# Gating layer of a decoder trunk: one column block of u computed with both parts of x as one moving operand

## The reference, cut to what matters

```python
def mixer_sgu(x, w_in, b_in, ln_g, ln_b, w_s, b_s, w_out):
    h = jax.nn.gelu(x @ w_in + b_in)               # (256, 2048)
    u, v = jnp.split(h, 2, axis=-1)                # 1024 columns each
    v = layer_norm(v, ln_g, ln_b)
    v = v.reshape(B, nc, SGU_CHUNK, SGU_GROUPS, gw)  # 2 chunks of 128 tokens, 8 groups of 128 channels
    w = jnp.where(causal, w_s, 0)
    mixed = jnp.einsum('gts,bcsgd->bctgd', w, v) + b_s.T[None, None, :, :, None]
    y = u * mixed.reshape(B, S, SGU_WIDTH)
    return y @ w_out
```

## Time and profile before

| what | us |
|---|---|
| median of three runs | 998.92 |
| the profiled execution's own time | 998.7 |
| its span in the trace | 997.0 |
| TensorE busy | 991.9 (99% of the span) |
| TensorE weight loads busy | 850.7 (85%) |
| VectorE busy | 703.7 (71%) |
| ScalarE busy | 458.3 (46%) |

### The profile page before, as it was taken

One profiled execution on the slowest core, in us unless ns is written; L12 is line 12 of the kernel. 1 busy time (PEld: TensorE's weight loads), 2 busy tenths in 40 slices (PEclk: granted clock), 3 DMA queues, 4 the chain that ended last, 5 costly groups with the idle time before them and its releaser, 6 DMA issues.

```text
span 997.0 us, 13952 instructions
## 1 busy us (share of the span) xinstructions
PE 991.9 (99%) x5370; PEld 850.7 (85%) x5370; DVE 703.7 (71%) x876; ACT 458.3 (46%) x524; POOL 49.7 (5%) x74
## 2 busy tenths in 40 slices
PE   9999999999999999999999999999999999999998
PEld 7888888889878888888888888888898888888887
DVE  5866666878678766666786666668787876666684
ACT  5444344246574544444445443434354553434441
POOL 0700000100001000000010000000210000000010
PEclk9999999999999999999999999999999999999999
DMA  8965656466264675555457755555466676565531
GB/s 289 289 234 168 211 168 212 133 191 185 85 212 164 201 245 192 188 191 194 143 170 270 230 183 201 180 199 182 145 205 218 215 243 213 168 212 171 211 128 43
DMA packets 129799, 191.45 MB, mean 192 GB/s; under 512 B 5448, under 2 KB 95816, under 8 KB 129760
## 3 DMA queue, kind: packets, MB, share of 16 engines
q1 hardware_dynamic: 126432, 180.11, 54.5%
q0 software_dynamic: 3040, 10.54, 3.1%
q10 hardware_dynamic: 288, 0.26, 0.1%
HBM read 189.83 MB, written 1.06 MB: 191 GB/s over the span
## 4 chain that ended last, share of the span: by engine, by line
PE 99%; DMA 0%; DVE 0%; issue 0%; DVEq 0%
PE gu L619 26%; PE gu L627 14%; PE acc L435 10%; PE acc L436 10%; PE acc L437 10%; PE gu L435 6%; PE gu L437 5%; PE gu L436 5%; PE tp L534 2%; PE gu L829 2%; PE gu L919 2%; PE gu L810 2%; PE gu L834 1%; PE gu L924 1%; PE gu L813 1%; PE acc L754 1%
## 5 line engine op out<-in xcount | busy, mean ns | idle before, releaser
L619 PE MATMUL gu<-xT,g_hi 128*128 128x512 f32 x1152 | 274.6, 390 | 0.0
L619 PEld LDWEIGHTS gu<-xT,g_hi 128*128 128x128 f32 x1152 | 215.5, 188 | 44.5 <-ACT g_hi L987 0.2
L1472 DVE TENSOR_REDUCE stage<-gu 128x256 f32<-128x512 f32 x72 | 49.8, 691 | 146.0 <-PE gu L627 146.0
L627 PEld LDWEIGHTS gu<-xT,g_lo 128*128 128x128 f32 x1152 | 147.7, 191 | 5.6
L627 PE MATMUL gu<-xT,g_lo 128*128 128x256 f32 x1152 | 149.4, 283 | 0.0
L1323 DVE TENSOR_TENSOR g_lo<-rawA,g_hi 128x2048 fp32r<-128x2048 f32 (+2 forms) x63 | 136.8, 2173 | 17.4 <-ACT g_hi L987 17.2
L1323 DVE TENSOR_TENSOR g_lo<-rawB,g_hi 128x2048 fp32r<-128x2048 f32 (+1 forms) x64 | 136.5, 2134 | 7.4 <-ACT g_hi L987 7.3
L435 PE MATMUL acc<-d_hi,hT_hi 128*128 128x512 f32 x352 | 138.6, 394 | 0.0
L436 PE MATMUL acc<-d_lo,hT_hi 128*128 128x512 f32 x352 | 137.9, 392 | 0.0
L437 PE MATMUL acc<-d_hi,hT_lo 128*128 128x512 f32 x352 | 137.0, 389 | 0.0
L987 ACT ACTIVATE g_hi<-rawA 128x2048 fp32r<-128x2048 f32 (+2 forms) x64 | 116.0, 1816 | 40.6 <-DMA rawA<-in_ffn_w_up 16.0
(11 more groups left out here) (205 smaller groups left out, 1020.9 us busy)
## 6 DMA issues: line engine op xcount, KB each, us to landing
rawD<-in_ffn_w_down SPq DMA_DIRECT2D x44, 1024.0 KB, 5.5
rawA<-in_ffn_w_gate SPq DMA_DIRECT2D x42, 512.0 KB, 4.0
rawA<-in_ffn_w_up SPq DMA_DIRECT2D x42, 512.0 KB, 5.0
rawB<-in_ffn_w_gate SPq DMA_DIRECT2D x42, 512.0 KB, 4.0
rawB<-in_ffn_w_up SPq DMA_DIRECT2D x42, 512.0 KB, 5.0
rawA<-in_attn_w_in SPq DMA_DIRECT2D x12, 512.0 KB, 4.4
rawB<-in_attn_w_in SPq DMA_DIRECT2D x12, 512.0 KB, 4.5
rawA<-in_ple_w_gate SPq DMA_DIRECT2D x8, 512.0 KB, 4.8
```

Of the source, the lines that this page charges most:

```text
L619: pe.matmul(bank[:, :], g_hi[:, slot, b, at:at + P], xT[:, b, :, :].rearrange("p i t -> p (i t)"), start=b == 0, stop=False)
L627: done = pe.matmul(bank[:, 0:S], g_lo[:, slot, b, at:at + P], xT[:, b, 0, :], start=False, stop=b == KB - 1)
L1472: dve.tensor_reduce(gates, gu[0][:, :].rearrange("p (i t) -> p t i", i=2), AXX, ALU.add).then_inc(gate_sum, 1)
```

## The change

The pieces n = 4 and n = 5 (chunk c = 2, the first column block of u) use a new function `u_wide`. It puts the two channel blocks of a piece into the two banks, and multiplies each high weight with both parts of x in one matmul of 512 columns; the low weights follow in a second pass of 256 columns. VectorE adds the halves of each bank (`u_sum`) into `stage`, and ScalarE's gelu reads `stage` (`gelu_sum`) and signals `u_ready`. The sums of n = 4 stand inside the norm of half 0, between its two steps; the sums of n = 5 and both low parts of chunk g0 + 3 stand ahead of the statistics of half 1. Pieces 6 and 7 stay as they were.

```diff
-           "sgu": dict(g=6, d=0, u=4, t=2, v=2, a=4, x=4, r=4, ln=2),
+           "sgu": dict(g=6, d=0, u=5, t=2, v=2, a=4, x=4, r=4, ln=2),
@@ tensor
+                    def u_wide(c, h):
+
+                        slot = (g0 + c) % 2
+                        for n, (wait, w) in enumerate((((high_a, high_b), g_hi), ((split_a, split_b), g_lo))):
+                            for i_b in range(2):
+                                if n == 0:
+                                    pe.wait_ge(gu_taken[i_b], u0 + c + h)
+                                at = P * (2 * h + i_b)
+                                for b in range(KB):
+                                    if h == 0 and i_b == 0 and b % 4 == 0:
+                                        pe.wait_ge(wait[b // 4], g0 + c)
+                                    if n == 0:
+                                        pe.matmul(gu[i_b][:, :], w[:, slot, b, at:at + P],
+                                                  xT[:, b, :, :].rearrange("p i t -> p (i t)"), start=b == 0, stop=False)
+                                    else:
+                                        done = pe.matmul(gu[i_b][:, 0:S], w[:, slot, b, at:at + P], xT[:, b, 0, :],
+                                                         start=False, stop=b == KB - 1)
+                                if n == 1:
+                                    done.then_inc((wide_full, g_done)[i_b], 1)
+
                     for n, (c, h) in enumerate((c, h) for c in range(4) for h in range(2)):
-                        bank_free(n % 2, u0 + n // 2)
+                        if n < 4:
+                            bank_free(n % 2, u0 + n // 2)
+                        elif n > 5:
+                            bank_free(n % 2, u0 + 4)
...
+                        elif c == 2:
+                            u_wide(c, h)
                         else:
                             u_product(c, h)
@@ scalar
+                    def gelu_sum(h):
+
+                        for i_b in range(2):
+                            act.wait_ge(gu_taken[i_b], u0 + 3 + h)
+                            done = act.activation(uT[:, 2 * h + i_b, :], stage[:, i_b, S * h:S * h + S],
+                                                  ACT.Gelu_apprx_tanh, bias=bu_col[:, 2 * h + i_b:2 * h + i_b + 1])
+                        done.then_inc(u_ready, 1)
+
-                    gelu_u(4)
-                    gelu_u(5)
+                    gelu_sum(0)
+                    gelu_sum(1)
@@ vector
-            def ln_apply_row(src, dst, h, ln, ready):
+            def ln_apply_row(src, dst, h, ln, ready, between=None):
...
                 steps[0] += 2
+                if between is not None:
+                    between()
                 dve.wait_ge(rstd_ready, 2 * ln + h + 1)
...
+                    def u_sum(h, i_b):
+
+                        dve.wait_ge(*((wide_full, 2 * WIDE + h + 1), (g_done, 2 * g0 + 5 + h))[i_b])
+                        if h == 0:
+                            dve.wait_ge(act_done, a0 + 3 + i_b)
+                        dve.tensor_reduce(stage[:, i_b, S * h:S * h + S],
+                                          gu[i_b][:, :].rearrange("p (i t) -> p t i", i=2), AXX, ALU.add)\
+                            .then_inc(gu_taken[i_b], 1)
+
+                    def u_sums():
+                        u_sum(0, 0)
+                        u_sum(0, 1)
...
-                        for bank in range(2):
-                            dve.wait_ge(gu_taken[bank], u0 + 3 + j)
+                        if j == 0:
+                            dve.wait_ge(u_ready, 2)
+                        else:
+                            for bank in range(2):
+                                dve.wait_ge(gu_taken[bank], u0 + 5)
...
                     ln_stats(v_sgu[:, 0, :], 0)
                     biased(3, 1)
-                    ln_apply_row(v_sgu[:, 0, :], v_sgu[:, 0, :], 0, ln0, vn_ready)
+                    ln_apply_row(v_sgu[:, 0, :], v_sgu[:, 0, :], 0, ln0, vn_ready, between=u_sums)
+                    lo_g(g0 + 3, 0)
+                    lo_g(g0 + 3, 1)
+                    u_sum(1, 0)
+                    u_sum(1, 1)
                     dve.wait_ge(act_done, a0 + 4)
                     ln_stats(v_sgu[:, 1, :], 1)
-                    lo_g(g0 + 3, 0)
-                    lo_g(g0 + 3, 1)
                     ln_apply_row(v_sgu[:, 1, :], v_sgu[:, 1, :], 1, ln0, vn_ready)
```

More of the change, by code:

```diff
@@ L277, in build @@
         wide_full = sem("wide_full")
+        u_ready = sem("u_ready")
         y_ready, y_high, y_low = sem("y_ready"), sem("y_high"), sem("y_low")
```

## The result

Twenty executions each: median 1000.49 us against 998.67 us before, 1.82 us more, a ratio of 1.0024 with a 95% interval of 1.0018 to 1.003. The forecast was 1000.4 us, 1.5 above the 998.92 that the first three executions of the kernel before had given; the range was 999.5 to 1001.5. The profiled execution took 1000.43 us, 1.7 more than the one before, and its span is 998.7 against 997.0.

A forecast was written before the change was run, and what follows sets the result against it. The prediction took TensorE, busy for 99% of the span, to bound the kernel. Its terms, -0.42 + 1.79 + 0.12 = +1.49 us, on 998.92 us gave 1000.4 us, with a range of 999.5 to 1001.5.

The forecast's parts named there:

- Part 1: Matmuls of n = 4 and 5: two pieces in the 512-column form save 0.42 us.
- Part 2: In n = 4, TensorE waits 1.68 us for biased(3, 1) to free bank 1, plus 0.11 restart: 1.79 us.
- Parts 3 and 4: From n = 4 to 5, waiting for bank 0 costs 0.12 us; from n = 5 to 6, mixing hides VectorE's work, cost 0.
- the tie of part 3: Ahead of n = 5, bank 0 is freed at 737.94 and TensorE wants it at 738.00; 0.12 us taken.
- Part 5: Behind n = 6: later norm, gate and w_out loads stay hidden, cost 0; g0 + 5's first half keeps 0.3 us cover.
- a late load of w_out: In the stage's later loads: a w_out load landing late would show the forecast wrong.
- n = 6 did not wait: Rival ahead of n = 6: a longer VectorE list makes bank 0 late, in sum +1.9 us, 1000.8 us; chance 0.12.
- the late-half rival: Rival at w_out: g0 + 5's first half lands late, +1.0 us, in sum +2.5, 1001.4 us; chance 0.16.
- The gain if the wait were gone: Rival in n = 4: bank 1 is free by 732.5, leaving -0.30 us, 998.6 us; chance 0.06.
- The sum: Whole kernel: saved matmul time, bank 1 wait and bank 0 restart, -0.42 + 1.79 + 0.12 = +1.49 us.
- The low end of the range: Whole kernel: stall 1.6, no bank 0 penalty, +1.1, less 0.5 for differing builds: 999.5 us.

The follow-up runs named there:

- experiment 8: Changed kernel with VectorE's biased(3, 1) and sums reordered, g0 + 4's first low part earlier, norm load later: 998.91 us; a mended order: 999.63 us.
- Experiment 1: Changed kernel with VectorE's biased(3, 1) moved ahead of the statistics of half 0: 999.16 us, and 999.22 us when run again.
- experiment 3: Changed kernel with the order inside u_wide turned round, bank 0 high and low, then bank 1 high and low: 999.85 us.
- experiment 4: Changed kernel with two more statistics instructions of 0.68 us each on VectorE ahead of the statistics of half 0: 1004.18 us.
- experiment 2: Changed kernel with biased(3, 1) moved ahead of the low part of the second half of chunk g0 + 2: 999.44 us.
- the changed kernel's second run: The changed kernel unaltered, run again on one chip beside other versions: 1000.67 us, ratio 1.0024 to the kernel before.
- experiment 6: Changed kernel with biased(3, 1) ahead of half 0's statistics and GpSimd's load of the next norm's parameters held back: 998.64 us.
- experiment 5: Changed kernel with biased(3, 1) ahead of half 0's statistics and g0 + 4's first low part ahead of the gate's first sum: 998.47 us, again 998.67.

## Why the prediction was right

**Part 1, the matmuls (-0.42).** The least disturbed two wide pieces take 11.19 us (experiment 8) against 11.52: 0.33 saved, with one restart of 0.1 in it, which is the forecast 0.42. By an estimate from the Trainium skill's cycles for an isolated matmul (TensorE: Matmul & The Clock Gate, "Back-to-back issue gap") it would have been 0.08; the runs side with the rows.

**Part 2, the bank asked for earlier (+1.79).** The step was right and named its releaser. The gap was 734.37 less 730.71 + 8 x 0.2275, 1.84 us, where 1.68 was forecast: `biased(3, 1)` ran 0.19 later than in the earlier trace rows, since the load ahead of it landed 0.2 later. The restart was 1.94 - 1.82 = 0.12. Experiment 1 took the gap away and 1.3 to 1.45 us with it, experiment 3 filled it in part, experiment 4 lengthened it. These three leave no other cause for the larger part of the loss.

**Parts 3 and 4 (+0.12 and 0).** 3.73 - 3.64 = 0.09, and no wait ahead of n = 6: bank 0 was free at 745.45, TensorE came at 745.57, a margin of 0.12 where 0.1 was forecast. The trace of experiment 2 confirms the tie of part 3: with a microsecond of standing still added early in VectorE's list, TensorE waits a microsecond there.

**Part 5 (0), right in the profiled execution, with hardly a margin.** VectorE's list went as forecast, to 0.2 us: norm of half 1 ended at 750.32 (750.1 forecast), low part of y started at 758.03 (757.85). The loads of w_out held TensorE up by nothing. But the danger was not in the first half of g0 + 5, where I had put it, but in the second, which I had not priced: issued at 756.80, it was in use at 763.76, its low part ended at 767.22 and TensorE came for it at 767.39. In the traces of the changed kernel's second run and of experiments 1 (again) and 2 TensorE waited 0.3 to 0.6 us for it. The prediction named a late load of w_out as a sign of being wrong, and in that second run it is there, with 0.33 us. In the kernel of experiment 1, taking it away lowered the median by 0.55 us. What it makes in the median of the changed kernel was not measured; the profiled execution has none of it and stands within 0.1 us of that median.

**The other rivals.** The wait was there, and n = 6 did not wait. The price of the late-half rival was taken from the 6.68 us of the half that shared its time with GpSimd's transfers; experiment 6 has 7.0 and 7.3 us without them, so its reason was wrong. The gain if the wait were gone was put at 0.3 below before: experiment 5 has 0.0 to 0.2 below, within its interval of no change.

**The sum** of the profiled execution, -0.42 + 1.96 + 0.09 + 0.05 for a later start, is 1.68 against 1.69 measured at the mixing. That the idle time in the trace is 1.69 as well is chance. Of the 1.82 us of the medians 1.49 were forecast; 0.17 more came from part 2 and 0.05 from the later start, 0.03 less from part 3. The 0.14 that is left is no more than single executions differ from their medians by: the two profiled ones stand 0.03 and 0.06 us off theirs, and 0.05 is lost behind the first product with w_out.

**Where luck helped.** The forecast time is off by only 0.1 us because two errors cancel: the change cost 0.3 us more than forecast, and 998.92, the median of three executions from which it was counted, is 0.25 us above that of twenty. The low end of the range was also added up wrong by 0.1: 1.6 - 0.42 is 1.18, not 1.1.

## What to carry to other kernels

A form that works with two banks at once asks for the second bank early, here 1.8 us after the first in place of a whole piece (5.8 us) later; before taking it over, look up what the releasing engine has ahead of that bank's release. A saving of 0.42 us on 32 merged matmuls is worth nothing if one instruction of another engine stands 1.6 us too late in its list, and an added instruction there also moves the loads that its neighbours set free. Where TensorE is 99% busy, compare where each edit's new request falls with where the other engine's list has got to, to a tenth of a microsecond.

## What was not expected

- A gap of 3.33 us on TensorE was followed by 4 us (737 to 741) with a granted clock that went down to 0.50 (experiment 4), one of 1.69 us was not (the changed kernel's profile stays at 1.00). All five executions with the longer gap have a mean clock of 0.997 to 0.999. What decides whether the clock falls, no run here shows.
- The changed kernel spreads more than the one before: 1000.12 to 1003.46 us in twenty executions against 998.27 to 999.35. Its chain runs through a load. Three of its four executions above 1002 us have a mean clock of 0.998 (the fourth, 1003.03, has 1.0), and in the second run the three slowest of ten, 1001.69 to 1003.07, have it. That a late load lengthened the gap until the clock fell fits experiment 4, but no trace of such an execution was taken, so it is argued and not shown.
- A half of w_out asked for 2.2 us after the other was in use 6.7 to 8.4 us after its issue, asked for 2.9 us or more after it in 6.4 or less. The end of a late one is thin: in the second run of experiment 1 the mean busy share of the DMA engines was 0.43, 0.33, 0.14 and 0.13 in the four half-microseconds from 760.5, in the second run of experiment 5 it was 0.49 and then 0. Whether a few of the 16 engines are late then or all of them run thinly was not looked into.
